# Later turns of probabilities, more task steps per latent piece, and a later scale root in a two-block transformer kernel

## The chip, the cores and the metric

The kernel runs on one core of one Trainium2 chip. The metric is the time of one execution on the device, in microseconds (us). Three timed executions of the kernel before gave 3256.42, 3256.81 and 3257.52 us; their median is 3256.81 us.

## The reference, cut to what matters

256 tokens of width 2048 pass through two blocks, everything in float32. What the change touches is three kinds of attention.

- In the first block a projection of the normed input gives a query latent of 512 columns, a key and value latent of 256 columns, one rotary key of 64 columns that all heads share, and the queries, keys and values of a banded attention. The *latent* attention (8 heads) multiplies the normed latents by `w_q_b` and `w_kv_b`, norms each head's query and key over 192 columns (128 plain, 64 rotary), turns the rotary part by the position (`rope`), and takes a causal softmax.
- The *banded* attention (16 heads of 64 columns, 2 key heads, a window of 128 tokens) adds a bias looked up by bucketed distance to the scores, and has a sink logit in each head's softmax.
- Then come the output projection `w_out`, a product-key expert layer (`peer_*`), whose gates are scattered into a table of 16384 x 256 floats in device memory that has to be zero beforehand, and the second block: its projection `w_in_2`, a differential attention, and a *neighbourhood* attention (8 heads of 128 columns, a bias per head and pair of tokens), gates, a branch sum, an output projection and an MLP.

## The kernel before

**Pieces.** All weights are cut into pieces of 128 x 1024 floats (512 KB), 1101 of them in one fixed order (`order`). A piece is loaded by SP's queue into one of 5 buffers (`raw`), split by ACT into a high part (`whi`, L1872) and by DVE into the rest (`wlo`, L2102), both with 3 buffers. TensorE (PE) multiplies it: 8 matmuls against `whi` and 4 against `wlo` in the pieces that the change touches (L1649). The split of piece n+2 is put into the streams of ACT and DVE just ahead of the matmuls of piece n.

**Order written out in advance.** One Python function, `walk`, sets the order of everything; each engine's program is what `walk` issues for it, and each engine runs its own instructions strictly in that order. Around the stream of pieces `walk` keeps lists of generators, `tasks` and `idle`: a *step* resumes every task once (and the first idle generator once), and each puts its next instructions into the streams. So what a step places for PE stands between two groups of matmuls, and PE waits there if it isn't ready. `gemm(...)` takes one step between two pieces of a product; with `mid=True` it takes one more in the middle of each piece, between the matmuls of its two halves.

**The latent stage.** The order of products is: `keys(0)`, `keys(1)` (a piece each), the second half of the banded queries (8 pieces, `swa_queries(1)`), `queries(2)` (2 pieces, the rotary columns), `values(0)`, `values(1)` (a piece each), `queries(0)`, `queries(1)` (2 pieces each). After each product ACT and DVE each copy half of the result out of PSUM (`evac2`, L1857 and L2190), and a task works on it: `k_nope` (squares on ACT, `k_scale`, `k_rows`, turns by PE, splits), `q_nope` and `q_rope` (squares on ACT L1958; for `q_rope` also `gain_rows` L2323 and `rope` L2177 to L2182 on DVE), `q_side` for the banded queries (square, `head_sum` L2155, `head_root`, `head_scale` L2166, turns). A *turn* is a group of four 128 x 128 transposes by PE (L1723) into one PSUM bank; ACT (`x_hi`) and DVE (`x_lo`, L2145 and L2148) then split the bank into `AA` or `BB`. `k_rope` turns the shared rotary key and spreads it twice over zeroed rows: POOL writes the zeros (`zero`, L2680), DVE spreads (`spread_kpe`, L2355), PE turns it. The second `zero` waits for the turns of the first. `q_scale` (L2334 and a chain of ten short instructions from L2077 to L2091 called `root`) gives the queries' scale, which only the softmax of the latent attention reads. The latent scores wait for the last `x_lo`.

**GpSimd's stream (POOL).** In this order: input loads, the zeros for the banded keys, the first `zero` of `k_rope`, `gate_blank` (a memset) and eight `gate_clear` DMAs of 2048 KB each that write the zeros of the gates' table (L2694), the second `zero` of `k_rope`, and `reload_x`, a DMA of 2048 KB that fetches `x` into `R` again after the latent attention (L2685). The first `scaled_residual` on DVE (L2373) waits for it.

**Attention units.** `attend` is one unit of scores and softmax: a step places the scores (PE), the next the maximum with the bias (DVE, L2211 to L2218) and the exponentials (ACT, L1914), the next the turn of the probabilities (PE, L1723), the next the copy of the turned bank (DVE L2236 and ACT in turns), the next the product with the values, the last the scaling by the row sum (`swa_out` L2311, `na_out`). Banded units (12, a new one every second step) run in the first 16 pieces of `w_out`, which use `mid=True`; neighbourhood units (8, two at a time) run among the gates' pieces of `w_in_2`, and the turns of their outputs follow. `row_factor` squares the latent output on ACT in that stretch (`group_squares`) and takes its root on DVE (`group_root`).

```python
def queries(j):                                                   # before
    pair, b, last = gemm("w_q_b", 2 * j, 4, BH, BL, nQ)
    ts, free = take(qrows)
    te = evac2(pair, b, last, lambda t: ts[:, t, :], free, t_lat, r=r_lat)
    tasks.append(q_nope(ts, te, j) if j < 2 else q_rope(ts, te, j))
    step()
```

Of the kernel before, what the change touches and what calls it, by code (L numbers as in the profile page):

```python
# [37 lines left out]
def build(nc, D, out):  # L38
# [12 lines left out]
    with ExitStack() as ctx:  # L51
# [51 lines left out]
        def heads(x, u):  # L103
            return x.rearrange("p (u l) -> p u l", u=u)
# [11 lines left out]
        sinks = GR[:, 384:400]  # L116
# [82 lines left out]
        def walk(steps):  # L199
# [3 lines left out]
            def go(step, *a):  # L203
                if step in steps:
                    steps[step](*a)

            def up(engine, name):
                count[name] = count.get(name, 0) + 1
                latest[engine] = (sem(name), count[name])
                return latest[engine]  # L210
# [292 lines left out]

            alt = [0]

            def attend(scores, U, nk, scale, sink, pslots, blocks, pv, finish, combine=None, per_head=None, added=None):
                bank, bfree = yield from wait_for(misc)
                tk = scores(bank, bfree)
                yield
                m, nm, sm, ri = stat(U), stat(U), stat(U), stat(U)  # L510
                if added is None:
                    go("row_max", bank, U, nk, m, nm, sink, scale, per_head, fresh("DVE", tk))
                    t1 = up("DVE", "row_max")
                    ps, pfree = yield from wait_for(pslots)
                    go("row_exp", banks[bank], U, nk, ps, nm, sm, scale, per_head, fresh("ACT", t1, pfree))
                    te = up("ACT", "row_exp")
                    misc.give(bank, te, t1)
                else:
                    ps, pfree = yield from wait_for(pslots)
                    go("biased_max", bank, U, nk, added[0], ps, m, nm, sink, fresh("DVE", tk, pfree, added[1]))  # L520
                    t1 = up("DVE", "row_max")
                    misc.give(bank, t1)
                    go("row_exp", ps, U, nk, ps, nm, sm, scale, None, fresh("ACT", t1))
                    te = up("ACT", "row_exp")
                ee, t4, t_exp = None, None, te
                if sink is not None:
                    es, ee = stat(U), stat(U)
                    go("sink_gap", es, sink, m, fresh("DVE", t1))
                    t3 = up("DVE", "sink_gap")
                    go("sink_exp", ee, es, fresh("ACT", t3))  # L530
                    t4 = up("ACT", "sink_exp")
                if combine is not None:
                    go("row_inv", sm, ee, ri, fresh("DVE", te, t4))
                    tr = up("DVE", "row_inv")
                    te = combine(ps, ri, [te, tr])
                    yield
                yield
                bank, bfree = yield from wait_for(misc)
                tk = transposed([ps[:, 128 * n:128 * n + 128] for n in range(blocks)], bank, te, bfree)
                pslots.give(ps, tk)  # L540
                yield
                pt, tfree = yield from wait_for(PT)
                alt[0] = 1 - alt[0]
                if alt[0] == 0:
                    go("copy_pt_a", pt, bank, blocks, fresh("ACT", tk, tfree))
                    tc = up("ACT", "pt_a")
                else:
                    go("copy_pt_v", pt, bank, blocks, fresh("DVE", tk, tfree))
                    tc = up("DVE", "pt_v")
                misc.give(bank, tc)  # L550
                yield
                bank, bfree = yield from wait_for(misc)
                tk = pv(bank, PTb[:, pt, :], [tc, bfree])
                PT.give(pt, tk)
                if combine is None:
                    go("row_inv", sm, ee, ri, fresh("DVE", t_exp, t4))
                    tr = up("DVE", "row_inv")
                yield
                misc.give(bank, finish(bank, ri, [tk, tr]))
# [205 lines left out]
            def swa_unit(t, h0):  # L765
                U = 2 if t else 4
                nk = 256 if t else 128

                def scores(bank, bfree):
                    assert len(qsw_t) == 4 and len(t_ksw) == 2 and len(bias_done) == 12  # L770
                    go("swa_scores", bank, t, h0, U, nk, fresh("PE", qsw_t, t_ksw, bfree))
                    return up("PE", "scores")

                def pv(bank, pt, toks):
                    go("swa_pv", bank, pt, h0, U, nk, fresh("PE", toks))
                    return up("PE", "weighed")

                def finish(bank, ri, toks):
                    go("swa_out", bank, t, h0, U, ri, fresh("DVE", toks, bias_done[-1]))
                    os_done[t, h0] = up("DVE", "swa_out")  # L780
                    return os_done[t, h0]

                def of_head(u):
                    return bias[:, h0 + u, 1:3, :] if t else bias[:, h0 + u, 0:1, :]

                return attend(scores, U, nk, 1.0, sinks[:, h0:h0 + U], psw, 4, pv, finish, added=(of_head, bias_done[-1:]))

            rq, rk = stat(16).rearrange("p (t h) -> p t h", t=2), stat(16).rearrange("p (t h) -> p t h", t=2)
            ssq, ssk = stat(32).rearrange("p (a t h) -> p a t h", a=2, t=2), stat(16).rearrange("p (t h) -> p t h", t=2)
# [5 lines left out]
            def squares(x, U, o, toks):  # L795
                k = sq_turn[0] = 1 - sq_turn[0]
                go("squares", x, U, o, k, fresh("ACT", toks, t_lat, sq_free[k]))
                sq_free[k] = [up("ACT", "squared")]
                yield
                return sq_free[k][0]  # L800
# [9 lines left out]
                qrows.give(ts, t_ssq, latest["PE"])  # L810

            def q_rope(ts, te, j):
                tr = []
                for t in range(2):
                    x = heads(ts[:, t, :], 8)
                    a = yield from squares(x, 8, ssq[:, 1, t, :], te)
                    t_ssq.append(a)
                    go("gain_rows", x, gq, 8, fresh("DVE", a, t_gr))
                    a = up("DVE", "gained")
                    yield  # L820
                    tr.append(rope(ts[:, t, :].rearrange("p (u c h) -> p u c h", u=8, c=2), 8, 32, CS[:, 0, t], CS[:, 1, t],
                                   [a, t_rope, x_read], Y[:, 0, 1024:2048]))
                    yield
                while not a_free:
                    yield
                yield from trans_split(lambda kt, t: ts[:, t, 128 * kt:128 * kt + 128], 4, hl(AH, 8), hl(AL, 8),
                                       None, tr, a_free, qt_done)
                qrows.give(ts, latest["PE"])

            def q_scale():  # L830
                while len(t_ssq) < 6:
                    yield
                yield
                go("q_scale", ssq, rq, fresh("DVE", t_ssq, latest["DVE"]))
                t_rq.append(up("DVE", "q_scale"))

# [46 lines left out]
            t_v = []  # L883

            def keys(j):
                pair, b, last = gemm("w_kv_b", j, 2, BH[:, 4:6, :], BL[:, 4:6, :], nKV)
                ts, free = take(krows)
                te = evac2(pair, b, last, lambda t: ts[:, t, :], free, t_kv, r=r_kv)
                tasks.append(k_nope(ts, te, j))
                step()  # L890

            def values(j):
                pair, b, last = gemm("w_kv_b", 2 + j, 2, BH[:, 4:6, :], BL[:, 4:6, :], nKV)
                t_v.extend(evac2(pair, b, last, lambda t: VM[:, t, 512 * j:512 * j + 512], x_read, t_kv, r=r_kv))
                step()
                return last

            def queries(j):
                pair, b, last = gemm("w_q_b", 2 * j, 4, BH, BL, nQ)
                ts, free = take(qrows)  # L900
                te = evac2(pair, b, last, lambda t: ts[:, t, :], free, t_lat, r=r_lat)
                tasks.append(q_nope(ts, te, j) if j < 2 else q_rope(ts, te, j))
                step()
# [445 lines left out]
            def na_unit(h):  # L1349
# [16 lines left out]
                def masked_first():  # L1366
                    go("na_mask", h % 2, fresh("DVE", nb_t[h]))
                    masked.append(up("DVE", "na_masked"))
                    yield
                    yield from attend(scores, 2, 256, 1.0, None, pslots, 4, pv, finish,  # L1370
                                      added=(lambda u: nbs[h % 2][:, 256 * u:256 * u + 256].rearrange("p (s k) -> p s k", s=2),
                                             masked))

                masked = []
                return masked_first()
# [1519 lines left out]
```

## Time and profile before

| what | value |
|---|---|
| median of three timed executions | 3256.81 us (3256.42 to 3257.52) |
| the profiled execution, its own time | 3259.14 us |
| its span | 3257.3 us |
| PE busy | 3200.2 us (98%) |
| DVE busy | 2106.2 us (65%) |
| ACT busy | 1517.7 us (47%) |
| POOL busy | 492.0 us (15%) |
| mean granted clock of PE | 0.994 of full speed |

All further times are those of the profiled execution, counted from the start of its span. Its own time is 2.33 us over the median, and 1.84 us of it lie around the span. Busy shares are averages over the whole program; the stretches that the change touches are 40 to 62 us (start), 93 to 167 us (latent stage), 209 to 293 us (banded units) and 2158 to 2275 us (neighbourhood units). A row of the timeline gives the start, the duration, the engine, the line, the operation, what it writes and reads, a count where instructions in a row are merged, and in brackets how long the engine sat idle before it and what ended that.

### The profile page before, as it was taken

The numbers are of one execution on the slowest core, as the hardware profiler recorded it, in microseconds if no ns is written. First come the engines' busy times: TensorE is split into PE (matmuls) and PEld (weight loads), VectorE is DVE, ScalarE is ACT, GpSimd is POOL, SyncE is SP. The second block draws the span as 40 slices with busy tenths as digits, with TensorE's granted clock in tenths as the row PEclk, the third lists the DMA queues.
The fourth block names the chain that finished last, engine by engine and source line by source line (L and its number), as shares of the span: only waits on it lengthen the run. The fifth ranks groups of instructions, "written<-read, shape, count | busy, mean of one in ns | idle before, by whom it ended". The sixth has DMA issues, their size and how long they took to land.

```text
span 3257.3 us, 40800 instructions
## 1 busy us (share of the span) xinstructions
PE 3200.2 (98%) x16112; PEld 2715.7 (83%) x16112; DVE 2106.2 (65%) x3062; ACT 1517.7 (47%) x2006; POOL 492.0 (15%) x322
## 2 busy tenths in 40 slices
PE   8989999999999999999999999999999999999998
PEld 7788888888888888888888888888888788888886
DVE  6766578887555576666666565565465655655556
ACT  5645454545444444444444544445444544444443
POOL 1000005777777200000000000000000000000000
PEclk9999999999999999999999999999999999999999
DMA  8623557888888866666665555444555455555554
GB/s 321 252 85 130 181 183 208 214 214 215 212 214 211 262 249 244 250 248 245 245 233 200 197 184 174 165 170 176 191 194 188 174 192 191 193 189 193 189 192 149
DMA packets 220286, 660.95 MB, mean 203 GB/s; under 512 B 56704, under 2 KB 56848, under 8 KB 217536
## 3 DMA queue, kind: packets, MB, share of 16 engines
q1 hardware_dynamic: 170864, 600.81, 52.9%
q0 software_dynamic: 49232, 57.54, 8.7%
q8 instruction: 127, 2.08, 0.3%
q14 instruction: 63, 0.52, 0.0%
HBM read 622.48 MB, written 35.78 MB: 202 GB/s over the span
## 4 chain that ended last, share of the span: by engine, by line
PE 90%; DVE 6%; ACT 2%; issue 1%; DMA 1%; DVEq 0%; ACTq 0%; SPq 0%
PE PS L1649 89%; DVE wlo L2102 2%; PE PS L1723 2%; ACT whi L1872 1%; DMA raw<-in_w_in_b 0%; DVE R L2606 0%; ACT M L1914 0%; DVE AA L2148 0%; ACT Y L1958 0%; DVE TMP L2177 0%; DVE M L2507 0%; DVE TMP L2178 0%; DVE BB L2148 0%; DMA R<-in_x 0%; DMA M<-in_na_bias 0%
## 5 line engine op out<-in xcount | busy, mean ns | idle before, releaser
L2102 DVE TENSOR_TENSOR wlo<-raw,whi 128x1024 fp32r<-128x1024 f32 x1101 | 1343.8, 1224 | 889.6 <-ACT whi L1872 878.4
L1872 ACT ACTIVATE whi<-raw 128x1024 fp32r<-128x1024 f32 x1101 | 1157.8, 1057 | 1033.4 <-PE PS L1649 998.3
L1649 PE MATMUL PS<-whi,AA 128*128 128x512 f32 (+1 forms) x2880 | 718.7, 390 | 2.0 <-DVE AA L2148 1.2
L1649 PE MATMUL PS<-whi,BB 128*128 128x512 f32 x2640 | 667.4, 393 | 1.7 <-DVE wlo L2102 1.2
L1649 PEld LDWEIGHTS PS<-whi,AA 128*128 128x128 f32 x2880 | 537.0, 189 | 112.4 <-DVE AA L2148 2.0
L1649 PE MATMUL PS<-BB,whi 128*128 128x512 f32 x2304 | 577.4, 392 | 1.7 <-DVE BB L2148 1.7
L1649 PEld LDWEIGHTS PS<-whi,BB 128*128 128x128 f32 x2640 | 491.1, 188 | 102.3 <-DVE wlo L2102 1.8
L2699 POOL DMA_INDIRECT scr_g<-M x256 | 446.9, 1746 | 426.4 <-issue 390.2
L1649 PEld LDWEIGHTS PS<-BB,whi 128*128 128x128 f32 x2304 | 414.4, 189 | 76.1 <-DVE BB L2148 1.9
L1649 PE MATMUL PS<-wlo,AA 128*128 128x512 f32 (+1 forms) x1440 | 389.4, 388 | 1.9 <-DVE wlo L2102 1.9
L1649 PE MATMUL PS<-wlo,BB 128*128 128x512 f32 x1320 | 356.3, 389 | 0.5 <-DVE wlo L2102 0.5
L1649 PEld LDWEIGHTS PS<-BB,wlo 128*128 128x128 f32 x2304 | 314.3, 190 | 22.5
L1649 PE MATMUL PS<-BB,wlo 128*128 128x256 f32 x2304 | 321.2, 282 | 0.0
L1649 PEld LDWEIGHTS PS<-wlo,AA 128*128 128x128 f32 x1440 | 271.2, 188 | 58.0 <-DVE wlo L2102 2.3
L1649 PEld LDWEIGHTS PS<-wlo,BB 128*128 128x128 f32 x1320 | 247.7, 188 | 53.1 <-DVE wlo L2102 0.9
L1649 PE MATMUL PS<-AA,whi 128*128 128x512 f32 (+1 forms) x1056 | 263.8, 391 | 2.6 <-DVE AA L2148 2.2
L1649 PEld LDWEIGHTS PS<-AA,whi 128*128 128x128 f32 (+1 forms) x1056 | 189.4, 188 | 37.2 <-DVE AA L2148 2.8
L1649 PEld LDWEIGHTS PS<-AA,wlo 128*128 128x128 f32 (+1 forms) x1040 | 141.8, 189 | 10.0
L1649 PE MATMUL PS<-AA,wlo 128*128 128x256 f32 (+1 forms) x1040 | 147.2, 282 | 0.0
L1857 ACT ACTIVATE AA<-M 128x512 fp32r<-128x512 f32 x72 | 45.5, 632 | 150.8 <-DVE M L2507 143.8
L1857 ACT ACTIVATE M<-TMP 128x512 f32<-128x512 f32 x64 | 40.5, 633 | 128.1 <-DVE TMP L2498 100.5
L2708 POOL DMA_DIRECT2D M<-scr_a x16 | 8.8, 547 | 589.8 <-DVE AA L2514 543.6
(236 smaller groups left out, 1570.0 us busy)
## 6 DMA issues: line engine op xcount, KB each, us to landing
raw<-in_peer_u SPq DMA_DIRECT2D x256, 512.0 KB
raw<-in_peer_v SPq DMA_DIRECT2D x256, 512.0 KB
raw<-in_w_in SPq DMA_DIRECT2D x160, 512.0 KB
raw<-in_w_up SPq DMA_DIRECT2D x128, 512.0 KB
raw<-in_w_down SPq DMA_DIRECT2D x128, 512.0 KB
raw<-in_w_out SPq DMA_DIRECT2D x64, 512.0 KB
raw<-in_w_in_a SPq DMA_DIRECT2D x32, 512.0 KB
scr_g<-M POOLq DMA_DIRECT2D x8, 2048.0 KB, 30.1
```

The lines of the kernel that those rows point to most:

```text
L1649: return e.matmul(outp, l, r, start=start, stop=stop)
L1723: last = e.transpose(banks[bank][:, 128 * n:128 * n + 128], s, ident)
L1857: e.activation(o, x, func, **kw).then_inc(sem(name), 1)
L1872: e.activation(whi[:, n % NH, :], raw[:, n % NR, :], ACT.Copy).then_inc(s_hi, 1)
L2102: e.tensor_tensor(wlo[:, n % NH, :], raw[:, n % NR, :], bf(whi[:, n % NH, :]), ALU.subtract).then_inc(s_lo, 1)
L2699: e.indirect_dma_start(out=D["scr_g"].rearrange("e (t o) -> (e t) o", o=1), out_offset=bass.IndirectOffsetOnAxis(ap=EID[t][:, k:k + 1], ax ...
L2708: e.dma_start(glt[i], D["scr_a"][sc, :, :]).then_inc(sem(f"gelu_fetched{i}"), 16)
```

## The change

1. `attend` gets a parameter `slack`: so many further steps lie between the exponentials and the turn of the probabilities. Banded and neighbourhood units pass `slack=1`; the latent and the differential units keep 0.
2. `keys`, `values` and `queries` call `gemm` with `mid=True`. A latent piece thus brings two steps of the tasks where it brought one.
3. `q_rope` places the squares of its two halves in two steps, and in the next step both `gain_rows` and both `rope`s together. Before, each half had its own steps: squares, then gain, then rope with the squares of the other half between.
4. `q_scale` is placed once all six `x_lo` of the queries are placed, not as soon as the six squares are.

```diff
-            def attend(scores, U, nk, scale, sink, pslots, blocks, pv, finish, combine=None, per_head=None, added=None):
+            def attend(scores, U, nk, scale, sink, pslots, blocks, pv, finish, combine=None, per_head=None, added=None, slack=0):
...
-                yield
+                for _ in range(1 + slack):
+                    yield
                 bank, bfree = yield from wait_for(misc)
                 tk = transposed([ps[:, 128 * n:128 * n + 128] for n in range(blocks)], bank, te, bfree)
...
             def q_rope(ts, te, j):
-                tr = []
+                xs, ta, tr = [heads(ts[:, t, :], 8) for t in range(2)], [], []
                 for t in range(2):
-                    x = heads(ts[:, t, :], 8)
-                    a = yield from squares(x, 8, ssq[:, 1, t, :], te)
-                    t_ssq.append(a)
-                    go("gain_rows", x, gq, 8, fresh("DVE", a, t_gr))
-                    a = up("DVE", "gained")
-                    yield
-                    tr.append(rope(ts[:, t, :].rearrange("p (u c h) -> p u c h", u=8, c=2), 8, 32, CS[:, 0, t], CS[:, 1, t],
-                                   [a, t_rope, x_read], Y[:, 0, 1024:2048]))
-                    yield
+                    ta.append((yield from squares(xs[t], 8, ssq[:, 1, t, :], te)))
+                t_ssq.extend(ta)
+                for t in range(2):
+                    go("gain_rows", xs[t], gq, 8, fresh("DVE", ta[t], t_gr))
+                    tr.append(up("DVE", "gained"))
+                for t in range(2):
+                    tr[t] = rope(ts[:, t, :].rearrange("p (u c h) -> p u c h", u=8, c=2), 8, 32, CS[:, 0, t], CS[:, 1, t],
+                                 [tr[t], t_rope, x_read], Y[:, 0, 1024:2048])
+                yield
                 while not a_free:
                     yield
...
             def q_scale():
-                while len(t_ssq) < 6:
-                    yield
-                yield
+                while len(t_ssq) < 6 or len(qt_done) < 6:
+                    yield
                 go("q_scale", ssq, rq, fresh("DVE", t_ssq, latest["DVE"]))
...
-                pair, b, last = gemm("w_kv_b", j, 2, BH[:, 4:6, :], BL[:, 4:6, :], nKV)
+                pair, b, last = gemm("w_kv_b", j, 2, BH[:, 4:6, :], BL[:, 4:6, :], nKV, mid=True)
...
-                pair, b, last = gemm("w_kv_b", 2 + j, 2, BH[:, 4:6, :], BL[:, 4:6, :], nKV)
+                pair, b, last = gemm("w_kv_b", 2 + j, 2, BH[:, 4:6, :], BL[:, 4:6, :], nKV, mid=True)
...
-                pair, b, last = gemm("w_q_b", 2 * j, 4, BH, BL, nQ)
+                pair, b, last = gemm("w_q_b", 2 * j, 4, BH, BL, nQ, mid=True)
```

`swa_unit` and `na_unit` end their call of `attend` with `slack=1`.

## Rows read from the trace of the kernel before

**Rows 1.** The page, part 1: busy time, share, instructions.

```profile
PE 3200.2 (98%) x16112; PEld 2715.7 (83%) x16112; DVE 2106.2 (65%) x3062; ACT 1517.7 (47%) x2006; POOL 492.0 (15%) x322
```

**Rows 2.** Waits of PE, whole span: us in total, times, longest.

```profile
PE PS L1723 <- ACT M L1914: 8.6, 7, 2.9
```

**Rows 3.** Timeline of PE, latent stage.

```profile
123.40 1.98 PE L1649 MATMUL PS<-whi,BB 128*128 128x512 f32 x8
126.12 0.60 PE L1723 MATMUL PS<-C,M 128*128 128x128 f32 x4
...
149.57 1.07 PE L1649 MATMUL PS<-wlo,BB 128*128 128x512 f32 x4
...
167.00 1.01 PE L1649 MATMUL PS<-BB,AA 128*128 128x256 f32 x3 [4.20 <-DVE AA L2148]
```

**Rows 4.** Timeline of DVE, latent stage.

```profile
131.78 1.21 DVE L2155 TENSOR_REDUCE ST<-TMP 128x16 f32<-128x1024 f32 x1
...
136.48 0.16 DVE L2077 TENSOR_SCALAR RT<-ST 128x16 f32<-128x16 f32 x1
...
138.44 0.75 DVE L2355 TENSOR_TENSOR M<-M,ST 128x256 f32<-128x256 f32 x2
139.12 0.69 DVE L2323 TENSOR_TENSOR M<-M,GR 128x512 f32<-128x512 f32 x1
...
140.85 0.74 DVE L2190 TENSOR_SCALAR R<-PS,ST 128x512 f32<-128x512 f32 x1
141.51 1.22 DVE L2166 TENSOR_TENSOR R<-R,ST 128x1024 f32<-128x1024 f32 x1
142.83 0.43 DVE L2177 TENSOR_TENSOR Y<-M,ST 128x256 f32<-128x256 f32 x1
...
144.98 2.35 DVE L2102 TENSOR_TENSOR wlo<-raw,whi 128x1024 fp32r<-128x1024 f32 x2
...
164.51 2.43 DVE L2148 SCALAR_TENSOR_TENSOR AA<-PS,GC,AA 128x256 fp32r<-128x256 f32 x6
```

**Rows 5.** Timeline of ACT, latent stage.

```profile
130.83 0.26 ACT L1958 ACTIVATE Y<-M 128x64 f32<-128x64 f32 x1
...
132.74 1.06 ACT L1872 ACTIVATE whi<-raw 128x1024 fp32r<-128x1024 f32 x1
```

**Rows 6.** Windows: length, busy of PE, PEld, DVE, ACT, POOL, PE clock, DMA share, GB/s.

```profile
168.00:171.00 3.00, 3.00 (x16) 3.00 (x15) 0.00 (x0) 0.00 (x0) 0.00 (x0) 0.50 0.00 0
...
230.00:235.00 5.00, 3.27 (x14) 3.17 (x15) 4.62 (x17) 2.69 (x10) 0.00 (x0) 0.55 0.16 66
```

**Rows 7.** Timeline of POOL, start to 240 us.

```profile
39.93 8.00 POOL L2694 DMA_DIRECT2D scr_g<-M  x7 [0.30 <-POOL M L2688]
105.00 1.12 POOL L2694 DMA_DIRECT2D scr_g<-M  x1 [57.07 <-issue]
154.68 0.95 POOL L2680 MEMSET M<- 128x1024 f32 x1 [48.56 <-PE PS L1723]
212.57 0.73 POOL L2685 DMA_DIRECT2D R<-in_x  x1 [56.95 <-DVE AA L2148]
```

**Rows 8.** Timelines of DVE and PE near 45 us.

```profile
43.42 3.77 DVE L2281 TENSOR_SCALAR TMP<-TMP 128x64 f32<-128x64 f32 x1
...
50.27 1.20 PE L1649 MATMUL PS<-wlo,AA 128*128 128x512 f32 x4 [1.86 <-DVE wlo L2102]
```

**Rows 9.** DMA queues, 52 to 56 us: packets, MB, share of 16 engines.

```profile
q0 software_dynamic: 252, 1.00, 94.4%
```

**Rows 10.** Timelines of PE and DVE, banded units.

```profile
231.73 1.12 PE L1723 MATMUL PS<-C,M 128*128 128x128 f32 x4 [2.86 <-ACT M L1914]
...
232.28 1.41 DVE L2373 SCALAR_TENSOR_TENSOR R<-PS,ST,R 128x512 f32<-128x512 f32 x2
...
279.95 0.65 PE L1723 MATMUL PS<-C,M 128*128 128x128 f32 x4 [1.24 <-ACT M L1914]
```

**Rows 11.** Waits of PE, 2105 to 2300 us.

```profile
PE PS L1723 <- ACT M L1914: 2.0, 3, 0.8
```

More of the change, by code:

```diff
@@ L784, in of_head @@
                     return bias[:, h0 + u, 1:3, :] if t else bias[:, h0 + u, 0:1, :]
-                return attend(scores, U, nk, 1.0, sinks[:, h0:h0 + U], psw, 4, pv, finish, added=(of_head, bias_done[-1:]))
+                return attend(scores, U, nk, 1.0, sinks[:, h0:h0 + U], psw, 4, pv, finish, added=(of_head, bias_done[-1:]), slack=1)
             rq, rk = stat(16).rearrange("p (t h) -> p t h", t=2), stat(16).rearrange("p (t h) -> p t h", t=2)
@@ L1371, in masked_first @@
                                       added=(lambda u: nbs[h % 2][:, 256 * u:256 * u + 256].rearrange("p (s k) -> p s k", s=2),
-                                             masked))
+                                             masked), slack=1)
                 masked = []
```

## The prediction, written before the run

> **What bounds the kernel now.** I read the page's busy shares first: PE is busy for 98% of the span [rows 1], so only what makes PE wait, or run slowly, can move the time by more than a few us. The waits of PE come next: the largest kind, 8.6 us in seven waits, are turns of probabilities that wait for ACT's exponentials [rows 2]. Third, the timelines of the latent stage: the last latent matmuls start at 149.57 and take 1.07, the latent scores start at 167.00 [rows 3]. In these 16.4 us PE does only turns, while DVE and ACT finish ropes, scales and splits. Fourth, the granted clock: after such a pause PE runs at 1.2 GHz for a while (0.50 of full speed from 168 to 171, a mean of 0.55 from 230 to 235) [rows 6], so a pause costs more than its length. Last POOL's timeline, since the change moves a step past queues: seven clearing DMAs are issued from 39.93 on, the eighth at 105.00, then POOL sits until the second zero at 154.68 [rows 7].
>
> **The change part by part.** All times are those of the profiled execution.
>
> *POOL's order.* With two steps per piece `k_rope` reaches its second `zero` inside `queries(1)`, ahead of `gate_blank` in POOL's stream; before, it came behind the clears. That zero waits for PE (the turns and the piece ahead of it, near 154). So all eight clearing DMAs move from 40 to about 156. At the old place something ends: DVE's scalar instruction on 64 columns at 43.42 took 3.77 us while POOL issued these DMAs, and PE then waited 1.86 us for `wlo` [rows 7, 8]. An instruction of that size needs about 0.2 (the ten of `root` take 1.96 [rows 4]), so this wait should go: **-1.9** (bounds -2.5 and 0).
>
> At the new place three things can suffer. DVE: its work beside the new issue time is mostly two-operand subtraction and evacuation; a delay like the one at 43.42 would be 3.6 us, or nothing; I take 0. The Trainium skill, SBUF — State Buffer, section Who interferes with whom, says that `tensor_scalar` in a two-port mode and GpSimd's writes exclude each other, but a `tensor_tensor` doesn't meet them. By that rule the sum here is 0, and the row at 43.42, a `tensor_scalar`, agrees with it. The position loads of the bias: 512 KB each beside the clears; +0.4 (0 to 2). And `reload_x`, below.
>
> *The latent stage.* Let t count from 123.40, the start of `queries(2)` [rows 3]; a piece takes 2.72, a turn about 0.45 (0.60 less what overlaps the next matmul). The steps now come twice as often, so DVE's side work comes earlier, and `q_side`'s turns stand right behind the third piece (`values(0)`). Until `head_scale` DVE has in its queue: an evacuation 0.74, two `wlo` 2.35, two rounds of gain and rope of the short key (seven short instructions each, 1.1 by `root`'s 0.2), two pairs of `x_lo` 1.6 (2.43 for six instructions), `head_sum` 1.21, `head_root` 1.96, a spread 0.75, a second evacuation 0.74, `head_scale` 1.22 [rows 4]: 12.8, and 0.9 in which it waits for ACT's first split. It ends at t = 13.7. PE has done three pieces and two turns at 9.1, and waits **4.6** for it.
>
> Next, `q_rope`'s squares wait for the second evacuation (t = 12.5); eight heads take 1.91 on ACT, the split behind them 1.06 [rows 5]. So DVE's `wlo` comes at 15.4 and ends at 16.6, then an evacuation, two `gain_rows` (0.69 each) and both ropes (142.83 to 144.98: 2.15 each) [rows 4]: 23.0. The turns of `q_rope` stand in the middle of `values(1)`, after two turns and a half piece for PE: 13.7 + 0.9 + 1.4 = 16.0. PE waits **7.0**. Before, both ropes were spread over six steps and PE waited for one of them only after the last piece.
>
> From t = 23.0 PE has four and a half pieces (12.2) and five turns (2.3): the last matmul ends at 37.5; before it was 150.64 - 123.40 = 27.2. Behind it ACT is the chain: evacuation 0.8, squares of four heads (between half of the 1.91 and all of it; 1.2), one plain and one scaled `x_hi` (0.5 and 0.75, taken from the `x_lo` pair), squares 1.2, three `x_hi` 2.25, and DVE's last pair 0.8: 7.5, up to 8.8 if ACT is late. The root of `q_scale` (1.96 and its add) now stands behind the last `x_lo`, beside the first scores. So the scores start at 45.0 to 46.3, against 43.6: +2.1. PE's first matmuls after the two waits will run at 1.2 GHz; the stretch after 167 [rows 6] suggests five to six us at that clock, 2.8 lost, of which ACT's slack gives back some 0.9. **+4.0**, bounds -2 (the clock holds, ACT keeps up) and +7.
>
> *Banded units.* Three waits at the start held PE for 8.6 - 2.0 - 1.2 = 5.4, the longest 2.86 [rows 2, 10, 11]. One step later is a half piece, 1.36, and the next unit's scores: the first two waits go. But the copy of the second unit's turn, on ACT, now stands behind the third unit's exponentials, and these behind `group_squares` and a split: I get 227.1 to 231.4 for PE, one wait of 4.3. -1.0. The wait of 1.24 at 279.95 goes, and part of the bank wait before it: -1.6. New at the end: the last unit's `swa_out` lies behind the fourth `scaled_residual`, which needs the piece's last matmul and takes 1.41 [rows 10]; the turn of that output stands ahead of the next piece: +1.9 with the `swa_out` itself. Together **-0.7**, bounds -5 (all waits go, the new ones hide) and +2.
>
> *`reload_x`.* From 52 to 56 the clears had the DMA engines nearly alone (94.4%) and moved 1.00 MB, 0.25 MB per us [rows 9]. POOL waited until 105.00 for its eighth issue, with all seven (14.7 MB) done [rows 7]. From 156 seven take 59 (at that rate) to 65 us (as from 39.93 to 105.00, with pieces beside them): 215 to 221. Then the eighth (8.4), and behind it on the same queue x, another 2 MB: landed at 232 to 238. DVE wants it near 234 (before: 232.28 [rows 10]), and everything behind `scaled_residual` on DVE, the next `wlo` and the next unit's maximum, waits with it; PE notices after about 1.8. **+1.0**, bounds 0 and +7. The Trainium skill, DMA: Bandwidth & Descriptors, section Anatomy of one DMA, gives a fixed 2 us and 436 GB/s: by it, as an estimate, seven would be done before 205, x would be in time, and the sum would be 1.0 lower. No row here shows that rate on this queue alone; the row at 52 to 56 is slower.
>
> *Neighbourhood units.* The three waits, 2.0 us [rows 11], go: a whole piece now lies between. Eight units, two at a time, of eight steps instead of seven: the turns of the outputs slip by four steps, three of them behind the last free gate piece, back to back; PE does them anyway, and two pieces are split ahead. **-2.0**, bounds -2.5 and +0.5.
>
> Sum: -1.9 + 4.0 + 0.4 - 0.7 + 1.0 - 2.0 = **+0.8** on 3259.14. The profiled execution lies 2.33 over the median; the forecast for a timed run is 3256.81 + 0.8 = **3257.6**: no change. I call 0.2%, 6.5 us, the least that this kernel's measurement can tell from none.
>
> **Rivals.** *A, faster.* DVE keeps up in the latent stage, so neither turn waits, and only the shorter tail counts: 7.5 instead of 16.4, less 1.3 for three turns that move ahead of it: -7.6, with the other terms -10.8: **3246.0**. For it: the old tail is PE's longest pause of the kernel [rows 3]. Against: 12.8 us of DVE's work stand in 9.1 us of PE's.
>
> *B, slower.* x lands late. For it: the rate of 0.25 MB per us and one queue for both [rows 7, 9]. If the position loads and the first pieces of `w_out` slow the clears further, POOL issues the eighth at 225 and x lands at 242; DVE stands for 8, PE for 6 of it, and its clock falls again (2.8 lost [rows 6]): +0.8 - 1.0 + 8.8: **3265.4**. It decides from the point at which x lands more than 1.8 after DVE asks. Against: no piece is split between the latent products and `w_out`, so the clears have less beside them than at the old place, where seven took 65.
>
> *C, only the units count.* POOL's order has no effect and the latent stage gives back what it takes: -2.7, **3254.1**; within the 0.2% too.
>
> **How the numbers follow.** Forecast 0.52, C 0.18, A 0.15, B 0.15. Forecast and C are no change: 0.70; A is faster, B slower. The range leaves out A's and B's outer parts: the terms' bounds taken together by halves give about -7.5 and +8: 3249.5 to 3265.5.
>
> **What would show it.** No clearing DMA before 150, the zero of the rotary key ahead of them; the short instruction of DVE near 43 below 0.3, and no wait of PE near 50. Two waits of PE between the third and the fifth piece of `w_q_b`/`w_kv_b` products, of 4 to 5 us (`head_scale`) and 6 to 8 us (the second rope), and a tail of 7 to 9 us. The eighth clear near 215, x landed near 235. One wait near 231 for a copy on ACT, one of about 1.9 near 292, none of the neighbourhood turns. It is wrong if PE passes `values(1)` without a wait, or if DVE stands at the first `scaled_residual` for over 3 us.

## The result and the profile after

| | before | after |
|---|---|---|
| median of 22 timed executions each, same chips | 3257.84 us | 3264.07 us |
| profiled execution, own time / span | 3259.14 / 3257.3 us | 3267.02 / 3265.2 us |

The ratio of the times is 1.0016, 95% interval 1.001 to 1.0022: 5.2 us slower (3.3 to 7.2). The two medians of the table lie 6.2 us apart. The time lies in the range that was forecast, and by the 0.2% it is "no change", at the upper edge of it; the sum said +0.8. The two profiled executions lie 7.9 us apart, and the ledger below is made of these: that of after lies 2.95 us over its median, that of before 1.3, and each kernel has one profile, so a stage's size can be off by a few us where its cause is not.

The page of the kernel after, part 1 [rows 1]:

```profile
PE 3203.6 (98%) x16112; PEld 2720.5 (83%) x16112; DVE 2101.5 (64%) x3062; ACT 1520.4 (47%) x2006; POOL 486.8 (15%) x322
```

The waits of PE over the whole span of after (us in total, times, longest). The line that led the list before, turns that wait for ACT's exponentials [rows 2], is gone; the lines shown are new or longer:

```profile
PE PS L1649 <- DVE AA L2148: 9.9, 6, 5.6
...
PE PS L1723 <- DVE M L2182: 5.6, 1, 5.6
PE PS L1649 <- ACT PTb L1857: 4.2, 1, 4.2
PE PS L1723 <- DVE R L2166: 4.2, 1, 4.2
PE PS L1649 <- DVE Y L2250: 3.3, 1, 3.3
PE PS L1723 <- DVE M L2355: 2.6, 1, 2.6
PE PS L1723 <- DVE Y L2311: 2.0, 2, 1.7
```

Where each of them stands: the timeline of PE in the latent stage of after [rows 3]. Four waits in a row, for `head_scale` (L2166), the second rope (L2182), the spread rotary key (L2355) and the last `x_lo` (L2148):

```profile
120.33 1.07 PE L1649 MATMUL PS<-whi,BB 128*128 128x512 f32 x4
...
133.74 1.97 PE L1723 MATMUL PS<-C,R 128*128 128x128 f32 x8 [4.20 <-DVE R L2166]
...
143.41 1.12 PE L1723 MATMUL PS<-C,M 128*128 128x128 f32 x4 [5.61 <-DVE M L2182]
...
159.44 0.66 PE L1723 MATMUL PS<-C,M 128*128 128x128 f32 x4 [2.57 <-DVE M L2355]
...
162.24 0.62 PE L1649 MATMUL PS<-wlo,BB 128*128 128x512 f32 x2
162.70 2.34 PE L1723 MATMUL PS<-C,M 128*128 128x128 f32 x20
170.65 1.01 PE L1649 MATMUL PS<-BB,AA 128*128 128x256 f32 x3 [5.61 <-DVE AA L2148]
```

The timeline of POOL of after [rows 7]: the second zero comes first, the clears behind it, the eighth at 209.27, `reload_x` at 221.67.

```profile
154.19 0.95 POOL L2680 MEMSET M<- 128x1024 f32 x1 [115.49 <-PE PS L1649]
155.09 0.31 POOL L2688 MEMSET M<- 128x256 f32 x1
155.69 8.00 POOL L2694 DMA_DIRECT2D scr_g<-M  x7 [0.30 <-POOL M L2688]
209.27 1.12 POOL L2694 DMA_DIRECT2D scr_g<-M  x1 [45.58 <-issue]
221.67 0.73 POOL L2685 DMA_DIRECT2D R<-in_x  x1 [11.27 <-DVE AA L2148]
```

**A ledger by landmarks.** Four rows of PE's timeline can be found in every kernel: the start of `queries(2)`, the first latent scores, the first matmul of `w_out`, and the first whole `w_out` piece behind the banded units. Their distances put each change of time in a stage (profiled executions, us):

| kernel | `queries(2)` starts | latent stage, to the scores | scores to `w_out` | banded stretch | rest, to the end |
|---|---|---|---|---|---|
| before | 123.40 | 43.60 | 42.50 | 83.06 | 2964.7 |
| after | 120.33 | 50.32 | 48.25 | 83.73 | 2962.6 |
| e1_clears_early | 122.45 | 50.56 | 42.05 | 81.99 | 2961.8 |
| e2_clears_late | 120.37 | 50.42 | 42.23 | 81.97 | 2961.6 |
| e3_before_clears_late | 119.14 | 43.58 | 41.59 | 82.87 | 2964.0 |
| e4_units_only | 123.04 | 43.56 | 42.65 | 82.68 | 2962.0 |
| e5_units_and_clears | 119.18 | 43.58 | 42.47 | 83.25 | 2962.0 |
| e6_two_steps_late | 120.03 | 44.03 | 41.82 | 81.99 | 2963.2 |
| e7_ropes_apart | 120.50 | 50.38 | 42.01 | 82.03 | 2961.8 |
| e8_one_step | 120.21 | 48.28 | 42.87 | 82.30 | 2962.0 |
| e9_after_squares_behind | 119.52 | 47.99 | 43.27 | 82.01 | 2961.6 |
| e10_group_squares_early | 119.48 | 43.58 | 42.46 | 80.47 | 2961.7 |
| e11_squares_behind | 119.24 | 44.30 | 43.49 | 82.00 | 2961.8 |
| e12_both | 119.92 | 43.15 | 42.90 | 79.50 | 2962.5 |

After against before: -3.1 + 6.7 + 5.75 + 0.7 - 2.2 = +7.9. (The last column is rounded, the sum is not.) Two stages lose, and the larger surprise is the second: from the latent scores to `w_out`, where the change put nothing but the root of `q_scale`, which e1 and e2 have there too.

### The profile page after: what moved, and what is told of

It is laid out like the page before. It is cut to its first block, busy times and chain, and to the rows that moved or that the text cites. A ratio compares the mean times of both kernels' runs of the same rounds, so it can differ in the third digit from the quotient of the medians.

```text
span 3265.2 us, 40796 instructions
## 1 busy us (share of the span) xinstructions
PE 3203.6 (98%) x16112; PEld 2720.5 (83%) x16112; DVE 2101.5 (64%) x3062; ACT 1520.4 (47%) x2006; POOL 486.8 (15%) x322
## 4 chain that ended last, share of the span: by engine, by line
PE 90%; DVE 6%; ACT 2%; issue 1%; DMA 0%; DVEq 0%; ACTq 0%; SPq 0%
PE PS L1649 89%; DVE wlo L2102 2%; PE PS L1723 1%; ACT whi L1872 1%; ACT M L1914 0%; ACT Y L1958 0%; DVE R L2606 0%; DMA R<-in_key_pos 0%; DVE M L2211 0%; DVE AA L2148 0%; DVE TMP L2177 0%; DVE M L2507 0%; DVE TMP L2178 0%; DVE BB L2148 0%; DMA R<-in_x 0%
```

## Experiments

Each was timed in five rounds beside the kernel before; medians and ratios to it:

| | median us | ratio (95%) |
|---|---|---|
| e1 | 3260.95 | 1.001 (1.0 to 1.0019) |
| e2 | 3258.92 | 1.0002 (0.9993 to 1.0011) |
| e3 | 3255.23 | 0.999 (0.9981 to 0.9999) |
| e4 | 3253.95 | 0.9987 (0.9978 to 0.9996) |
| e5 | 3251.22 | 0.9978 (0.9969 to 0.9987) |
| e6 | 3252.16 | 0.9981 (0.9972 to 0.999) |
| e7 | 3257.78 | 0.9998 (0.9989 to 1.0007) |
| e8 | 3256.69 | 0.9992 (0.9983 to 1.0001) |
| e9 | 3257.68 | 0.9998 (0.9989 to 1.0007) |
| e10 | 3249.28 | 0.9972 (0.9961 to 0.9983) |
| e11 | 3253.67 | 0.9984 (0.9975 to 0.9993) |
| e12 | 3250.78 | 0.9976 (0.9967 to 0.9985) |

The kernel before had 3258.31 us beside e1 to e4, 3258.9 beside e5 to e8 and 3258.89 beside e9 to e12.

### Where the clears stand: e1, e2, e3

e1 puts `gate_blank` and the eight `gate_clear` ahead of `queries(0)` in the changed kernel's walk, so that they pass the second zero in POOL's stream. e2 (on the changed kernel) and e3 (on the kernel before) put them behind the banded units, with a wait:

```diff
             while idle:
                 step()
+            go("gate_blank")
+            t_blank = up("POOL", "gate_blank")
+            for c in range(8):
+                go("gate_clear", c, fresh("POOL", t_blank, half_sum[-1]))
+                t_clear = landing("gate_cleared")
```

> The changed kernel with the blank and the eight clearing DMAs put ahead of the second zero of the rotary key in POOL's stream again, as in the kernel before. Theory (the clears' new place holds the position loads of the bias): the early gain of 3.1 us at the start of queries(2) is lost (start near 123.4), but the key positions land in about 4 us again, the wait of 3.3 us for above_sel near 210 goes with the slow clock behind it, and the stretch from the first latent scores to the first w_out matmul falls from 48.3 to about 42.5 us (-5.8). Net -2.7 against the changed kernel: some 2.5 us slower than the kernel before, ratio 1.0008. Rival (DVE's own order in the latent attention makes above_sel late, the clears don't): the stretch stays at 48 and only the early loss shows: 8 us slower than before, ratio 1.0025. The latent stage itself stays at about 50 us from queries(2) to the scores by both, unless POOL's issue of the clears near 156 to 164 slowed DVE there: then the wait of 2.6 us for the spread key near 159 shrinks.

> The changed kernel with the clears behind the banded units: they wait for the last half sum of w_out, near 290 us, and run beside the last w_out pieces and the expert layer's first ones. Theory: the early gain of 3.1 us stays, the position loads are free, the stretch from the scores to the first w_out matmul is near 42.5: 5.8 us less than the changed kernel, about level with the kernel before (ratio 1.0000, profile span near 3259.5). Rival 1 (DVE's order makes the position wait): no different from the changed kernel, ratio 1.0016. Rival 2 (clears always cost where they run): 3 us or more come back between 290 and 370 us as waits of PE for wlo or whi, or a DVE scalar instruction of 4 us.

> The kernel before with nothing changed but the clears, which wait for the last half sum of w_out near 290 us. Theory: DVE's scalar instruction of 3.8 us near 43 falls to 0.2, PE doesn't wait for wlo near 50, and queries(2) starts near 120.3 instead of 123.4; nothing else changes: 3.1 us faster than the kernel before, ratio 0.9990. Rival (the early gain of the changed kernel came from its other steps, or is given back at the next wait for data): less than 1 us, ratio 0.9998 to 1.0000.

Measured: the stretch from the scores to `w_out` is 42.05 and 42.23 with the clears anywhere else, against 48.25: the theory holds in both, the rival (DVE's own order) falls. The chain can be read in after. The four loads of key positions share two buffers. SP's timeline: the first load of the second pair waits until DVE has read that buffer, and is issued at 200.88.

```profile
200.88 0.33 SPq L2753 DMA_DIRECT2D R<-in_key_pos  x1
```

The DMA view of after from 196 to 212 us (KB each, us from issue to landing), and the same line of e2 (3.2 in before, 3.1 in e1):

```profile
R<-in_key_pos SPq DMA_DIRECT2D x1, 512.0 KB, 8.2
```

```profile
R<-in_key_pos SPq DMA_DIRECT2D x1, 512.0 KB, 3.3
```

DVE of after waits for that landing, PE for DVE, and PE then runs slowly:

```profile
209.12 1.28 DVE L2250 SCALAR_TENSOR_TENSOR Y<-POS,C,R 128x1024 f32<-128x1024 int32 x1 [2.89 <-DMA R<-in_key_pos]
```

```profile
210.46 7.09 PE L1649 MATMUL PS<-ST,Y 128*128 128x64 f32 x32 [3.33 <-DVE Y L2250]
```

Windows of after (busy times of PE, PEld, DVE, ACT, POOL, then PE's granted clock, DMA share, GB/s), and of e2, where the matmuls of after's first row run from about 206.8 to 212.2:

```profile
206.00:216.00 10.00, 6.67 (x37) 6.44 (x36) 5.98 (x9) 0.84 (x2) 1.12 (x1) 0.64 0.84 302
216.00:224.00 8.00, 8.00 (x34) 7.07 (x34) 4.25 (x7) 3.00 (x6) 0.73 (x1) 0.60 0.24 71
```

```profile
200.00:210.00 10.00, 9.40 (x83) 9.02 (x82) 9.84 (x17) 1.80 (x5) 0.00 (x0) 1.00 0.49 160
210.00:218.00 8.00, 7.62 (x50) 6.92 (x51) 7.29 (x13) 3.57 (x6) 1.04 (x2) 1.00 0.12 18
```

PE's waits for `above_sel` (L2250) are 3.3 us in after and 1.0 in e2, so of the 6.0 us between the two some 2.3 are the wait and 3.7 the clock. A clock of 1.00 is 2.4 GHz; in windows of 2 us, after has 0.50, that is 1.2 GHz, in each from 210 to 222, while e2 has 1.00 throughout. The low clock reaches into the next stage: the first two half pieces of `w_out` take 4.47 us in after and 2.83 in e2, another 1.6. PE's timelines, after and then e2:

```profile
218.90 2.05 PE L1649 MATMUL PS<-whi,AA 128*128 128x512 f32 x4
...
223.37 1.05 PE L1649 MATMUL PS<-M 128*128 128x128 f32 x8
```

```profile
213.02 1.17 PE L1649 MATMUL PS<-whi,AA 128*128 128x512 f32 x4
...
215.85 1.05 PE L1649 MATMUL PS<-M 128*128 128x128 f32 x8
```

The timing says the same with a smaller size: e2 is 0.6 us slower than the kernel before, after 5.2, so moving the clears away gives some 4.6 us timed, where the two profiles lie 8.6 apart.

The early part: with the clears at their old place (before, e1, e4) `queries(2)` starts at 122.5 to 123.4, in all others at 119.1 to 120.5. In e3, where only the clears moved, that is the whole gain in the early part. e1 brings the slow scalar instruction back; after and e2 don't have it. The timeline of DVE, e1 and then after [rows 8]:

```profile
42.42 3.77 DVE L2281 TENSOR_SCALAR TMP<-TMP 128x64 f32<-128x64 f32 x1
```

```profile
40.55 0.20 DVE L2281 TENSOR_SCALAR TMP<-TMP 128x64 f32<-128x64 f32 x1
```

Rival 2 of e2 (clears cost wherever they run) falls too: from 290 to 400 us PE is busy for 106.62 us in e2 and 106.61 in after. e1's timed loss of 2.6 us is what it was expected to be, and e2's 0.6 is level. For e3 the spans differ by 6.1 us, the timing by 3.1 (0.3 to 6.2): the profiled execution of before happens to lie 0.8 over the median timed beside e3, that of e3 2.2 under its own, so the timing is the better figure.

### The units alone: e4, e5

e4 is the kernel before with change 1 and nothing else. e5 adds the late clears of e3.

> The kernel before with slack=1 in the banded and the neighbourhood units and nothing else of the change. Theory (ledger of the two profiles): the banded stretch from the first w_out matmul to the last banded turn is about level (+0.7: three waits of 5.4 us go, but a wait of 4.2 us for the copy of a turned bank on ACT and a slow clock come), the neighbourhood stretch gains 2.0: 1.4 us faster, ratio 0.9996. Rival (the banded wait and its slow clock are what makes the changed kernel slower): the banded stretch is 4 us or more longer, ratio 1.0008 or above.

> The kernel before with the later turns in both kinds of units and with the clears that wait for the last half sum of w_out; the latent stage is that of the kernel before. Theory (the terms add up: e3 gave 3.1, e4 4.4 timed): 7 us faster than the kernel before, ratio 0.9978; the latent stage takes 43.6 us from queries(2) to the scores as before. Rival (both gain from the same slack, a wait that moves back): 4 to 5 us, ratio 0.9986.

The rival of e4 falls: units alone are faster by 4.2 us (1.3 to 7.2; the 1.4 expected is at the edge of that), with the gain where it was expected, in the neighbourhood stretch (rest: -2.8; no wait of PE between 2140 and 2310 us, against three before [rows 11]). The banded stretch is level. It has one long wait where before it had several, the wait that the prediction worked out; PE's timeline in e4 (whose lines behind the edit are numbered one higher) and in after:

```profile
231.97 1.97 PE L1650 MATMUL PS<-M,PTb 128*128 128x64 f32 x8 [4.21 <-ACT PTb L1858]
```

```profile
242.72 1.80 PE L1649 MATMUL PS<-M,PTb 128*128 128x64 f32 x8 [4.21 <-ACT PTb L1857]
...
302.22 0.66 PE L1723 MATMUL PS<-C,Y 128*128 128x128 f32 x4 [1.70 <-DVE Y L2311]
```

e5 is 7.2 us faster than before (4.2 to 10.1), so the timing alone leaves room for the 4 to 5 us of its rival; the ledger shows both gains in full, -4.2 at the start and -2.7 in the rest: they add.

### The latent stage: e6, e7, e8

e7 is e2 with the old `q_rope`; e8 is e2 without any `mid=True` in the latent products; e6 is e5 with the late root and this:

```diff
-                pair, b, last = gemm("w_q_b", 2 * j, 4, BH, BL, nQ)
+                pair, b, last = gemm("w_q_b", 2 * j, 4, BH, BL, nQ, mid=j < 2)
```

> As e5_units_and_clears, with the scale's root last and two steps per piece in queries(0) and queries(1) alone; keys, values and queries(2) keep one step and q_rope keeps its halves apart. Theory (two steps cost where the turns overtake DVE's chain of square, sum, root and scale and q_rope's squares, at queries(2) and the values, and pay at the end): no wait for head_scale, a shorter tail than 17.4 us (10 to 13), the stage 39 to 42 us instead of 43.6, so 2 to 4 us less than e5. Rival (any doubled step makes PE wait, since DVE and ACT are the ones that are late): waits of 3 us or more for q_rope or the spread key inside queries(0) and queries(1), the stage at 44 to 47.

> e2_clears_late with q_rope's halves in their own steps again; two steps per latent piece and the late root stay. If it is the joint ropes that hold PE (5.6 us at q_rope's turns): that wait shrinks by 3 us or more, since the turns stand three steps later, and the stage falls from 50.4 to 46 or 47. If it is the doubled steps (ACT's squares and DVE's chain simply aren't done): the wait only moves to the next turns, the stage stays at 49 to 51.

> e2_clears_late with one step per latent piece again; the joint ropes and the late root stay. If the doubled steps make the stage long: no wait of 4.2 us for head_scale, the stage falls from 50.4 to 43 us or less, since the joint ropes bring q_rope's turns ahead of the tail and the root leaves it: some 7 us less than e2, ratio to the kernel before 0.9980. If the joint ropes do: a wait of 4 us or more stays in front of q_rope's turns and the stage is at 46 or more.

I had thought that the doubled steps alone lengthen the stage. e7 agrees (50.38, no change). e8 does not: with one step per piece, the joint ropes and the late root make it 48.28, with one wait of 8 us, which is for the second rope; the root stands behind that rope in every kernel. PE's timeline in e8, then in e7:

```profile
144.71 1.11 PE L1723 MATMUL PS<-C,M 128*128 128x128 f32 x4 [8.00 <-DVE M L2182]
```

```profile
146.64 1.12 PE L1723 MATMUL PS<-C,M 128*128 128x128 f32 x4 [4.08 <-DVE M L2182]
```

Either edit brings `q_rope`'s turns ahead of the last pieces, before DVE has the second rope. Counted from `queries(2)`, that rope is done 23.1 us on in after, 24.5 in e8, 26.1 in e7, 30.6 before: the edits do make it earlier, but PE asks for it earlier still (17.5 in after, 27.2 before). In e6 PE waits 3.8 us for it, behind `queries(0)`, 1.75 for the spread key and 1.5 for `head_scale`, which its theory had ruled out, and 5.6 at the end: the shorter tail is paid for, the stage is 44.03, and e6 is no faster than e5. The rival of e6 holds, at its lower end.

### Two ways to better it: e9 to e12

e9 (on e2) and e11 (on e6) put the squares of the plain query columns behind their turns:

```diff
             def q_nope(ts, te, j):
-                for t in range(2):
-                    t_ssq.append((yield from squares(heads(ts[:, t, :], 4), 4, ssq[:, 0, t, 4 * j:4 * j + 4], te)))
+                for _ in range(2 * (1 - j)):
                     yield
...
                                        lambda kt: GC[:, 88:89], te, a_free, qt_done)
+                for t in range(2):
+                    t_ssq.append((yield from squares(heads(ts[:, t, :], 4), 4, ssq[:, 0, t, 4 * j:4 * j + 4], te)))
```

e10 is e5 with the two squares of `row_factor(OM, ...)` one step earlier (its delay 4 instead of 5, and one more step ahead of the root).

> e2_clears_late (the changed kernel, clears behind the banded units) with the squares of the plain query columns behind their turns instead of ahead of them. In the changed kernel eight squares (2.4 us with a split between) stand on ACT from 155.2 to 158.5, the split of the next piece behind the first four, DVE's rest of that split behind it and the spread of the rotary key behind that; PE waits 2.6 us for the spread, a wait that the prediction left out. Theory: without the squares in front the wait falls below 0.5 us, and the tail from the last latent matmul to the scores falls from 8.4 to 6 us, since four squares of 1.2 us twice leave ACT's chain there: the stage from queries(2) to the scores falls from 50.4 to 45.5 us. Rival (the spread waits for POOL's zero or for DVE's own work, not for ACT): the wait of 2.6 stays, only the tail is shorter, 48 us.

> e5_units_and_clears with the two squares of row_factor (1.06 us each and their sums, 2.3 us on ACT) one step earlier, in an idle stretch of ACT ahead of the second banded unit's exponentials, and the root where it was. Theory: ACT's chain (second unit's exponentials, group squares, split, third unit's exponentials, copy of the second unit's turned bank) made PE's wait of 4.2 us near 224 to 228; without the squares in it the wait falls to about 2, bounded by the third unit's scores and maximum, and the clock falls for a shorter stretch: 2 to 3 us faster than e5, the stretch from the first w_out matmul to the full pieces at 80.5 instead of 83.2. Rival (the third unit's maximum on DVE sets the copy's time): the wait stays at 3.5 to 4.2, no gain.

> e6_two_steps_late with the squares of the plain query columns behind their turns. Theory: the tail falls from 8.4 to 6 us, and the split of the pieces in queries(0) and queries(1) is no longer behind squares: the stage at 40 to 41.5 us instead of 44.0, some 3 us less than e6 and 2 less than e5. Rival (the root of the scale, now later, holds the softmax; or the waits move to q_rope's turns): the stretch behind the scores grows by what the tail loses, no gain over e6.

> e11_squares_behind and e10_group_squares_early together. Theory: the two gains lie in different stretches and add: 3246.5 to 3248 us, ratio 0.9965 to 0.997 to the kernel before, 11 us. Rival (the clock, which falls after each wait, or the banded units take the gain back): no better than e5, ratio 0.9978.

e9 lies between its theory and its rival. The wait for the spread key falls from 2.57 to 1.40 us, not to 0.5, and the stage to 47.99, the 48 of the rival: 1.2 us of the wait were squares on ACT, the rest is the chain of evacuation, split and rest that remains. In after that chain reads so, ACT and then DVE (squares from 155.24, the split behind them, then DVE's rest and the spread):

```profile
155.24 0.31 ACT L1958 ACTIVATE Y<-M 128x128 f32<-128x128 f32 x1
...
156.41 1.05 ACT L1872 ACTIVATE whi<-raw 128x1024 fp32r<-128x1024 f32 x1
```

```profile
157.49 1.23 DVE L2102 TENSOR_TENSOR wlo<-raw,whi 128x1024 fp32r<-128x1024 f32 x1 [1.42 <-ACT whi L1872]
158.63 0.76 DVE L2355 TENSOR_TENSOR M<-M,ST 128x256 f32<-128x256 f32 x2
```

e11 missed: its stage is 44.30, no shorter than e6's 44.03, and the stretch behind the scores is 1.7 us longer, as its rival said. e10 hit: PE's wait falls from 4.2 to 1.75 us and the banded stretch to 80.47. PE's and ACT's timelines in e10: the squares now fill a gap of ACT ahead of the exponentials.

```profile
226.12 1.10 PE L1650 MATMUL PS<-M,PTb 128*128 128x64 f32 x8 [1.75 <-ACT PTb L1858]
```

```profile
215.92 1.06 ACT L1858 ACTIVATE TMP<-Y 128x1024 f32<-128x1024 f32 x1
...
218.35 0.40 ACT L1915 ACTIVATE M<-M,ST 128x128 f32<-128x128 f32 x1
```

e12 missed too (3250.78 for at most 3248): it does not add e11's gain, which wasn't one. e10 is the fastest run, 3249.28 us: 9.1 us under the kernel before (5.5 to 12.7), and faster than the changed kernel. It keeps only change 1 of the four, with the clears out of the way. Its lead over e5 is within the timing's interval; the profiles show it as 2.8 us, all in the banded stretch.

## Why the prediction was right or wrong, step by step

| step | forecast | profile | |
|---|---|---|---|
| clears leave the start | -1.9 | -3.1 | mis-sized |
| position loads | +0.4 (0 to 2) | +5.75, and 1.6 behind it | wrong |
| latent stage | +4.0 (-2 to +7) | +6.7 | one wait missed |
| banded units | -0.7 | +0.7 (-1.1 in e1 and e2) | right, but for the loads' clock |
| `reload_x` | +1.0 | 0 | did not occur |
| neighbourhood units | -2.0 | -2.2 | right |

**The step that failed** is "The position loads of the bias: 512 KB each beside the clears; +0.4 (0 to 2)". It sets no landing of a load against the time at which DVE wants it. But two buffers serve four loads: the first load of the second pair is issued when DVE has read its buffer, at 200.88, and wanted at 206.23 (209.12 less the wait), so a landing of more than 5.4 us is on the path. It took 8.2 us beside the clears against 3.3 without them, DVE stood for 2.89, PE for 3.33, and the clock made it 5.75, with 1.6 more in the first pieces of `w_out`. e1 and e2 show it twice. The DMA queues of after from 170 to 200 us (packets, MB, share of 16 engines) show how little is left beside the clears:

```profile
q0 software_dynamic: 2517, 10.00, 97.4%
```

The Trainium skill, DMA: Bandwidth & Descriptors, section Queues, rings and completion order, says that each engine alternates between its queues packet by packet. By that, as an estimate, a load beside a queue that is never empty takes twice its time alone, 6.6 us; the run agrees in kind, with 8.2.

**The latent stage.** The two waits that were forecast came, 4.2 for 4.6 and 5.6 for 7.0, and the tail is 7.8 us (from 162.86, the end of the last matmul, to 170.65) for 7.5 to 8.8. The step "From t = 23.0 PE has four and a half pieces (12.2) and five turns (2.3): the last matmul ends at 37.5" has no wait in it; the run had 2.6 there, for the spread key, and the end at 42.5. The spread had been looked at only where it stood before, next to the zero. e9 shows what holds it: ACT's squares in part, and for the rest the splits. The remaining 2.4 us of that step are mostly PE's slow clock behind the second wait (0.50 from 143 to 147 us), which the prediction counted apart. PE's granted clock there stands third from the end:

```profile
143.00:147.00 4.00, 3.59 (x11) 3.01 (x12) 1.49 (x3) 0.00 (x0) 0.00 (x0) 0.50 0.35 129
```

The clock itself needed no term: the stage less its waits is 32.3 us in both kernels (43.6 less 4.2 + 3.3 + 2.8 + 0.5 + 0.5, and 50.3 less 5.6 + 5.6 + 4.2 + 2.6), since before the long tail of turns ran slowly too (a clock of 0.57 from 155 to 163). PE's timeline of before:

```profile
153.96 0.66 PE L1723 MATMUL PS<-C,M 128*128 128x128 f32 x4 [3.32 <-DVE M L2182]
...
157.02 5.78 PE L1723 MATMUL PS<-C,M 128*128 128x128 f32 x28 [2.40 <-DVE M L2355]
```

The stage grew by just what its waits grew, 6.7, and the 1.9 that the forecast had for the clock did not come. That is so for this pair and no rule: for the same matmuls PE is busy for 32.2 us of the stage in before and 32.4 in after, but for 31.0 in e6 and 34.4 in e7, whose waits are 1.9 us less than e2's while its stage is as long.

**The early start** lost two waits for `wlo`, 2.2 us together, and the prediction counted the longer one; the first x came 0.3 earlier. The starts of `queries(2)` in kernels of one kind differ by up to 1.4 us, so the rest can't be told from that.

**Banded units.** The wait of 4.3 forecast for the copy on ACT is 4.21, that of 1.9 at the end 1.70, and the wait of 1.24 at 279.95 [rows 10] is gone. The loss of 0.7 in after isn't theirs: 1.6 of it is the low clock that the position loads left. With the clears elsewhere (e1 and e2) the stretch is 1.1 shorter than before's, near the forecast. On the kernel before, without the other changes, the units leave it level (e4 -0.4, e5 +0.2); what makes that difference isn't shown.

**`reload_x`.** x was issued at 221.67 and landed in 9.5 us, at 231.2. The rate of the clears was guessed too low: from 170 to 200 the queue moved 10.00 MB, 0.33 MB per us and not 0.25, and the eighth went out at 209.27, not from 215 on. And the stage before had itself become 9.4 us later, so DVE asked for x later, too: the first `scaled_residual` at 242.70 waits for nothing. Even at before's time of asking, 232.28, x would have been there. Rival B's time of 3265.4 is near the measured one, but its mechanism did not occur; what came late was the key positions. The Trainium skill's rate (DMA: Bandwidth & Descriptors, section Anatomy of one DMA), by which, as an estimate, seven clears would be done before 205, was too high here: 0.33 MB per us is 333 GB/s, below the skill's 436.

So the verdict of "no change" held at its edge, and in part by luck (the interval reaches 0.22%, and the range ends 1.4 us above the measured median), while the sum was off by 7 us in the profiled executions (4.4 timed): 5.4 from the loads, 2.7 from the latent stage, 0.4 net from banded units and `reload_x`, less 1.4 at the start and in the neighbourhood units. The range does not follow from its own rule either: the terms' bounds reach 12.8 below and 17.7 above the terms, and by halves that is 3251.2 to 3266.5, not 3249.5 to 3265.5; the measured 3264.07 lies in both.

What stays open: no order tried here makes the latent stage shorter than before's 43.6 by more than 0.5 us (e12). Whether another order of ACT's and DVE's work could was not tried. How much the landing of the loads varies between executions isn't known, since each kernel has one profile.

## What to carry to other kernels

When an edit lets one step pass others in a queue, list everything that now runs beside the steps left behind: a load that reuses a buffer has its landing time on the path as soon as that is longer than the time from the buffer's release to its next use (here 8.2 us against 5.4), however small its bytes. Where DVE and ACT set the length of a stage, placing the tensor engine's turns earlier only moved its waits in the orders tried here; forecast the sum of the waits from the moment each operand is ready, for every operand that is asked for, not only for those whose code was edited. A long wait made of several short jobs can be shortened by moving the one that has a gap to go to, as the group squares in e10; in e11 the moved squares gained nothing.

## What the hardware showed that was not expected

A wait of 3.3 us in a stretch of small matmuls cost another 3.7 us in clock (after against e2), more than itself, and 1.6 behind the stage. And POOL's issue of the clears slows not one instruction of DVE but the first five of the group at the old place: in e1 the conversion at its head takes 0.69 us and the rows between it and the 3.77 us one 1.12 to 1.13, while after has 0.16 to 0.39 (the two of L2276 merged). At the new places no slow instruction is seen: the scaled evacuation at 162.90 in after, while POOL still issued, took 0.75 us, against 0.74 at 140.85 before [rows 4]. The Trainium skill, SBUF — State Buffer, section Who interferes with whom, names copies, casts and `tensor_scalar` as the kinds that can enter the mode that shuts GpSimd out or is shut out by it; the slowed instructions are of these kinds.
